# A hybrid GLA and convolution block on 8 cores: unequal halves of a sequence, with one plan of work for each half

## The reference

```python
p = h @ w_in[l]                                   # (B,S,IN_WIDTH)
q, k, v, g, lr, cb, cc, cx, ga, gb = jnp.split(p, SPLIT_IDX, axis=-1)
log_a = jax.nn.log_sigmoid((lr @ w_gate_up[l] + b_gate[l]).astype(jnp.float32)) / GATE_TAU
o = gla_chunked(qh, kh, vh, lah)                  # S_t = diag(a_t) S_{t-1} + k_t^T v_t ; o_t = q_t S_t
y_a = (rmsnorm(o, gla_norm_w[l]) * jax.nn.silu(g)) @ w_proj_a[l]
y_b = (cb * causal_depthwise_conv(cc * cx, conv_w[l])) @ w_proj_b[l]
z = jax.nn.sigmoid(ga) * y_a + jax.nn.sigmoid(gb) * y_b
x = x + gate1[:, None, :] * (z @ w_out[l])
m = jnp.square(jax.nn.relu(h2 @ w_mlp1[l])) @ w_mlp2[l]
x = x + gate2[:, None, :] * m
return rmsnorm(x, final_norm_w)
```

## Time and profile before

| | us |
|---|---|
| median of 3 runs | 1322.65 (1319.77 to 1343.83) |
| profiled execution | 1321.02 |
| its span, slowest core (5) | 1319.5 |
| spans of all cores | 1312.9 to 1319.5 |
| PE busy | 1250.9 (95%) |
| DVE, ACT, POOL busy | 751.3, 441.7, 89.4 |

### The profile page before, as it was taken

One profiled execution on the slowest core, in us unless ns is written; L12 is line 12 of the kernel. 1 busy time (PEld: TensorE's weight loads), 2 busy tenths in 40 slices (PEclk: granted clock), 3 DMA queues, 4 the chain that ended last, 5 costly groups with the idle time before them and its releaser, 6 DMA issues.

```text
span 1319.5 us, 19276 instructions; the slowest of 8 cores (1312.9 to 1319.5 us)
## 1 busy us (share of the span) xinstructions
PE 1250.9 (95%) x6772; PEld 611.2 (46%) x6772; DVE 751.3 (57%) x1203; ACT 441.7 (33%) x936; POOL 89.4 (7%) x133
## 2 busy tenths in 40 slices
PE   1588999999999999999999999999999999999996
PEld 1244565555554444444444444444444444444443
DVE  2468627767666565433232326676665556655786
ACT  2576526766431111331111113643111111112333
POOL 2000002244400000000000000000000000000000
PEclk9989999999999999999999999999999999999998
DMA  9568401001645353411113146004303023031122
GB/s 178 135 172 234 129 14 65 1 1 42 104 73 97 69 108 73 88 32 33 33 34 61 34 112 208 0 1 80 64 0 65 15 50 64 1 64 33 65 96 96
DMA packets 18173, 93.19 MB, mean 71 GB/s; under 512 B 2352, under 2 KB 2448, under 8 KB 12192
## 3 DMA queue, kind: packets, MB, share of 16 engines
q0 software_dynamic: 8208, 54.56, 22.8%
q1 hardware_dynamic: 9728, 37.14, 8.0%
q10 hardware_dynamic: 144, 0.26, 0.1%
HBM read 135.93 MB, written 8.39 MB: 109 GB/s over the span
## 4 chain that ended last, share of the span: by engine, by line
PE 91%; DMA 3%; DVE 2%; ACT 2%; issue 2%; POOL 0%; DVEq 0%; ACTq 0%; POOLq 0%
PE psf L429 88%; DMA wsl<-w_ada 3%; PE psf L439 2%; ACT Bt L374 1%; DVE Bx L422 1%; ACT hT L415 0%; DVE tmp L381 0%; ACT hT L374 0%; ACT tmp L374 0%; DVE S L396 0%; DVE x L381 0%; DVE h32T L384 0%; DVE x L396 0%; POOL xb L498 0%; DVE scb L381 0%
## 5 line engine op out<-in xcount | busy, mean ns | idle before, releaser
L429 PE MATMUL psf<-hT,wsl 128*128 128x512 bf16 x2944 | 661.0, 380 | 2.5 <-ACT hT L415 1.7
L429 PEld LDWEIGHTS psf<-hT,wsl 128*128 128x128 bf16 x2944 | 287.4, 98 | 344.2 <-issue 9.4
L374 ACT ACTIVATE tmp<-psf 128x512 f32<-128x512 f32 (+1 forms) x232 | 135.1, 582 | 532.1 <-PE psf L429 530.8
L429 PE MATMUL psf<-wsl,aT 128*128 128x512 bf16 (+1 forms) x1032 | 225.7, 379 | 2.0 <-DVE aT L381 2.0
L429 PEld LDWEIGHTS psf<-wsl,aT 128*128 128x128 bf16 x1032 | 101.2, 98 | 123.6 <-issue 4.8
L381 DVE TENSOR_TENSOR aT<-tmp 128x512 bf16<-128x512 f32 x128 | 88.6, 692 | 118.5 <-ACT tmp L374 113.3
L381 DVE TENSOR_TENSOR tmp<-tmp,psf 128x512 f32<-128x512 f32 (+1 forms) x72 | 45.2, 628 | 152.9 <-ACT tmp L374 152.9
L381 DVE TENSOR_TENSOR x<-x,tmp 128x512 f32<-128x512 f32 (+1 forms) x161 | 110.7, 688 | 16.8 <-DVE tmp L381 2.9
L381 DVE TENSOR_TENSOR tmp<-psf,g2b 128x512 f32<-128x512 f32 x129 | 88.6, 687 | 30.8 <-PE psf L429 30.8
L390 POOL TENSOR_SCALAR S_bf<-S,dec 128x256 bf16<-128x256 f32 x60 | 56.6, 960 | 184.9 <-DVE S L396 184.8
L429 PE MATMUL psf<-ogT,wsl 128*128 128x512 bf16 x256 | 60.5, 379 | 0.0
(11 more groups left out here) (170 smaller groups left out, 1045.3 us busy)
## 6 DMA issues: line engine op xcount, KB each, us to landing
wsl<-w POOLq DMA_DIRECT2D x16, 1024.0 KB, 9.0
wsl<-w_ada POOLq DMA_DIRECT2D x12, 1024.0 KB, 11.6
xb<-x_cur SPq DMA_DIRECT2D x16, 512.0 KB, 5.9
wsl<-w_merge POOLq DMA_DIRECT2D x8, 1024.0 KB, 8.4
x<-x_cur SPq DMA_DIRECT2D x16, 512.0 KB, 11.3
out<-x SPq DMA_DIRECT2D x15, 512.0 KB, 2.6
xb<-x_prev SPq DMA_DIRECT2D x12, 512.0 KB, 6.3
wsl<-w_conv POOLq DMA_DIRECT2D x8, 768.0 KB, 12.3
```

Source lines behind the costliest of these rows:

```text
L374: P.op("act", lambda e: e.activation(out=out, in_=in_, func=func, **kw), r, w, cost=0.19 + 0.00083 * size(in_) + (0.2 if "accum_out" in kw ...
L429: ins = e.matmul(out=o, lhsT=l, rhs=rh, start=st, stop=sp_)
```

## The change

- The halves are 17 and 15 subtiles (`SUBS`). `x_cur`, `x_prev` and `out` have 17.
- `record` gets `first` and is called twice; each result is planned by itself, and each engine's program holds both. An engine loads the word `half` from memory into a register and branches: half 0 (cores 0, 2, 4, 6) runs the first plan, half 1 the second.
- First plan: 17 subtiles in tiles of 4, 4, 3, 3, 3. No pass over x_prev, no `s0_pieces`: the state and the convolution's edge are set to 0 by POOL. x_cur tile 0 is loaded in the place of x_prev tile 0. Four weight buffers. k and q come once, in float32, on POOL's queue behind the four ada weights, and are cast on the chip by 8 pieces each on ACT or DVE (`cast`). Subtile 0 keeps its float32 q, k and scores, and its bf16 columns are no longer computed. In tile 0 all k products stand ahead of all q products, and v comes last. x tile 1 is loaded on POOL's queue.
- Second plan: 15 subtiles in tiles of 4, 4, 4, 3, and a pass over 17 subtiles in tiles of 4, 4, 3, 3, 3. Five weight buffers. No float32 q and k. No multiplication with the flag.
- Matmuls and vector work have the tile's own width (512 or 384). Buffers of the tiles are laid out anew; x1 is one buffer a subtile.
- The planner's assumed costs: x 1.9 (1.7), weights 6.1 a full one (6.5), the bus free from 6.0, small DMAs off it; and where no operation can go on, one whose engine could be chosen may go to the other.
- The chains gates, ln and scan of the first tile go head by head, not in pairs.

```diff
-TOK = 2048
-NW = 5
+SUBS = (17, 15)
@@
-        bus = 0.0
+        bus = 6.0
+        stuck = False
...
+                if cost < 1.0:
+                    end = st + 2.2
+                else:
+                    bus = max(bus, st + 1.0) + cost
+                    end = bus + 1.0
@@
+        def record(P, place, first):
+            main = tiles((4, 4, 3, 3, 3) if first else (4, 4, 4, 3), False)
+            past = [] if first else tiles((4, 4, 3, 3, 3), True)
+            seq = past + main
+            NW = 4 if first else 5
...
+                if first and name in ("k", "q"):
+                    return
...
+            def cast(name):
+                j, w32 = (4, w32k) if name == "k" else (5, w32q)
+                keys = [("w", j % NW)] + [("cast", name, kc) for kc in range(8)]
+                for kc in range(8):
+                    AV(wsl[j % NW].t[:, kc * 512:(kc + 1) * 512], w32.t[:, kc, :],
+                       w32.k((kc * 512, 512)) + [("free", j % NW)], [keys[1 + kc]])
+                return keys
...
             for j in range(4):
                 rec_load(j)
-            rec_load(4)
+            if first:
+                for dst, name, sem in ((w32k, "k", "c6"), (w32q, "q", "c5")):
+                    P.op("pool", lambda e, dst=dst, name=name: e.dma_start(
+                        out=dst.t[:, :, :].rearrange("p k c -> p (k c)"), in_=W[name][0]), [], dst.k(), dma=sem, cost=6.1)
+            else:
+                rec_load(4)
...
-            xload(1, after=[("w", 3)])
+            if first:
+                done_w(4)
+                xload(seq[1], eng="pool")
+            else:
+                xload(seq[1], after=[("w", 3)])
...
+            if first:
+                wkk = cast("k")
+                special_front()
...
+                    MM([(p_[:, w0:w], wk_[:, kc, hs], h_.t[:, kc, w0:w], kc == 0, kc == 7) for kc in range(8)], wkk + h_.k(), pk)
...
+            if first:
+                P.op("pool", lambda e: e.memset(S32.t[:, :, :], 0.0), [], S32.k())
+                P.op("pool", lambda e: e.memset(S_bf[0].t[:, :, :], 0.0), [], S_bf[0].k())
+                run(dense(main[0]))
...
             run(w1_stage(0, 0))
+            for t in range(1, NT):
+                tr2(main[t])
+                if t + 1 < NT:
+                    o_stage(main[t + 1])
+                if t + 2 == NT:
+                    done_w(2)
+                if t < 3:
+                    run(w1_stage(0, t))
             P.op("sp", lambda e: e.dma_start(out=fnw.t[:, :], in_=fnwb_d), [], fnw.k(), dma="c4")
+            todo1 = [(0, t) for t in range(3, NT)] + [(qd, t) for qd in range(1, 4) for t in range(NT)]
+            todo2 = [(qd, t) for qd in range(4) for t in range(NT)]
+            run(w2_stage(*todo2.pop(0)))
+            while len(todo1) > 1:
+                run(w1_stage(*todo1.pop(0)))
+                while len(todo2) > len(todo1) + 1:
+                    run(w2_stage(*todo2.pop(0)))
...
+                half = e.value_load(half_d[0:1, 0:1])
+                with e.If(half == 0):
+                    go(progs[0])
+                with e.Else():
+                    go(progs[1])
```

More of the change, by code:

```diff
@@ L125, in schedule @@
                         other = engs[1 - engs.index(e)]
-                        if max(free[other], ready[i]) < st + (MARGIN if e == engs[1] else 0.0):
+                        if max(free[other], ready[i]) < st + (MARGIN if e == engs[1] else 0.0) and not stuck:
                             continue
@@ L239, in k, with __init__, tiles @@
         return out
+class Tile:
+    def __init__(self, i, s0, n, prev):
+        self.i, self.s0, self.n, self.w, self.prev = i, s0, n, 128 * n, prev
+def tiles(widths, prev):
+    out, s0 = [], 0
+    for i, n in enumerate(widths):
+        out.append(Tile(i, s0, n, prev))
+        s0 += n
+    return out
 def plan():
@@ new lines, in dense @@
+                if nn:
+                    out.append((0.01, lambda: xload(nn)))
+                tr = [tr_piece(nx, kc) for kc in range(8)] if nx else []
+                if not (first and T.i == 0):
+                    for h in range(4):
+                        out += [q_piece(T, h), k_piece(T, h), vs.pop(0), ktr(T.i % 2, h, T)]
+                        out += tr[2 * h:2 * h + 2] if T.i else []
+                out.append((0.01, lambda: done_w(2 if nx is None else 0)))
+                if nx is None:
+                    return out + vs
@@ new lines, in dense @@
+                gs = gate_pieces(nx)
+                norm = sq_pieces(nn) if nn else []
+                rest = (tr if T.i == 0 else []) + [lr_piece(nx)] + gs[0:2] + norm[0:2] + gs[2:4] + norm[2:]
+                k_ = max(1, (len(rest) + len(vs) - 1) // len(vs))
+                while vs or rest:
+                    out += rest[0:k_] + vs[0:1]
+                    rest, vs = rest[k_:], vs[1:]
+                return out + (xs_pieces(nn) if nn else [])
+            if first:
+                P.op("pool", lambda e: e.memset(S32.t[:, :, :], 0.0), [], S32.k())
+                P.op("pool", lambda e: e.memset(S_bf[0].t[:, :, :], 0.0), [], S_bf[0].k())
+                run(dense(main[0]))
+            else:
+                for j in range(len(past) - 1):
+                    Vtt(ks[:, :], ksp[:, 0:4] if j == 0 else ks[:, :], ksp[:, j * 4 + 4:j * 4 + 8], ALU.add,
+                        [("ksp", 0), ("ksp", j + 1), "ks"], ["ks"])
+                d0 = dense(main[0])
+                run(d0[0:12])
+                weave(d0[12:], s0_pieces())
@@ L1347, in build_nc @@
+        progs = []
+        for first in (True, False):
+            planned = Prog()
+            record(planned, None, first)
+            order, place = planned.schedule({"ps": (8, 1), "tmp": (NTMP, 1)})
+            P = Prog()
+            record(P, place, first)
+            P.emit_all(order)
+            progs.append(P)
+        sem_names = sorted(set(progs[0].sems()) | set(progs[1].sems()))
         S = {n: es.enter_context(nc.semaphore(n)) for n in sem_names}
```

767 lines of the change are left out of this document (396 added, 371 removed).

## The result

The changed kernel takes 1279.66 us (median of 4 executions, 1279.23 to 1301.8) against 1321.77 of the kernel before in the same comparison: a ratio of 0.969, 95% interval 0.967 to 0.971. The profiled execution took 1279.36 us, with a span of 1277.7 on core 6. The forecast was 1285, range 1270 to 1302, and a span of 1283.

A forecast was written before the change was run, and what follows sets the result against it. TensorE was taken as the bound: a first-half main part of 1225.9 us beginning at 56 gives 1281.9, plus 1 for the jump, span 1283; with 1.5 outside the span 1284.5, called 1285, range 1270 to 1302.

The forecast's parts named there:

- the main part of 1163.1: Kernel before, from the first q product of the own tokens at 156.37 us to the span's end, nearly pure PE.
- Start: First-half opening: branch 2.5 us, hT ready at 46.8, first k product at 51, main part in effect from 56.
- the 5 us for half clock and first waits: First-half start: 5 us (0 to 12) added because the main part no longer begins with all weights there.
- Steps 1 to 5: First-half main part: 40.5 us stays, 16.6 goes, 1106.0 grows by 17/16 (+69.1), dropped columns -3.5, extra matmuls +1.3.
- Step 6: Tile boundaries in q, k, v and GLA: narrow tiles cover the vector chain less, +4 us (0 to 19).
- R1: Rival: vector chain bounds q, k, v and GLA with narrow tiles, 4.7 us a boundary, +15, 1300; chance 0.12.
- Step 7: MLP, first quarter: with four weight buffers one w2 load waiting for w_out's buffers is exposed, +8.5 us (0 to 14).
- R3: Rival: slower than before, four buffers uncover the MLP loads, six more exposures of 8.5 us, +51, 1336; chance 0.06.
- Jump at the end: End of the first-half program: 1 us for jumping over the other plan.
- The second half: Second-half cores: pass 117 us, main part from 169 lasting 1079, end at 1248, hidden behind the first half.
- the bound of 3.8: Start on every core: upper end for the register load and branch, two constants' landings, range 0 to 3.8 us.

The follow-up runs named there:

- the casts: Changed kernel with the pieces of the k and q casts alternating between ACT and DVE, q's after the first tile's scans: ratio 0.961, profiled first-half mean 1272.9 us.
- two gains: Changed kernel with both the alternating casts and the second half's start held by eight POOL fills: ratio 0.964, profiled first-half mean 1272.0 us.
- plans exchanged: Changed kernel with the two plans in swapped places in the program, each core doing the same work: ratio 0.972, profiled first-half mean 1287.3 us.
- held core 5: Second-half core of the changed kernel with the second half's first x request held by eight POOL fills: ratio 0.965, profiled first-half mean 1273.3 us.

## Why the prediction was right, and where it wasn't

The structure held: first-half cores set the end, the main part of 1163.1 grows by a sixteenth of what depends on tokens, and begins some 103 us earlier. The span of 1283 was 5.3 too long. By the steps:

- **Start.** Register and near branch cost 1.5 us (0 to 3.8, taken 2.5). hT was ready at 42.2, not 46.8: I kept the 37.9 us from the x request (1.57 to 39.48), and it became 34.2 because the neighbour core asks later. k landed 4.6 earlier for the same reason (6.4 us behind the fourth weight, where I took 6.5), but its cast took 7, not 2.5 (one engine instead of two), so the first k product came at 52.15 against 51. Two errors cancelled. Of the 5 us for half clock and first waits behind it, about 1.3 came (granted 0.97 over 45 us).
- **Steps 1 to 5** held. Two weight requests in the merge are now 29.41 us apart (491.47 and 520.88), and 27.62 x 17/16 is 29.35. 64 of 384 columns take 10.40 (807.24 to 817.64), 162.5 ns each, against my 163.
- **Step 6.** 6.2 us of waits in this stretch, against 5.2 (the 1.2 of before and 4 for the boundaries). It comes to 1.5 a boundary and not 4.7, so R1 didn't come. What I missed is which tiles make it: it is the run of 3-wide tiles, and 4,4,4,3,2 has 2.1. With the clock behind the waits and the tail, that run cost this change 8 us.
- **Step 7 is the step that fell.** 8.5 us for an exposed w2 load; measured 0. The release of an aT buffer gates only the vector product that writes it, so 40 matmuls of the next stage were free to move ahead, the end of my range that I gave to the planner. With them held back the kernel is 5 to 6 us longer, about what the step priced, but the wait was for the norm chain, which the step doesn't have. R3, which multiplied this step, had nothing under it: PE was busy 410.00 of 410.00 us in the MLP.
- **Jump at the end.** 1 us was allowed and 1.2 came, inside the span: 4.3 us from the last store request to its end, against 3.1 on far cores. The far branch itself, of which the prediction said that no run showed it, was left without a price at the second half's start.
- **The second half.** Main part from 169.59, predicted 169, end 1250.3, predicted 1248; but by two errors of the same size. Its start came 7.5 later (54.27 against 46.8), since the far branch is outside the bound of 3.8 that I set from the landing of the constants, and its pass took 115.3 us, not 122.2. Had the second half set the end, that bound would have been a costly one.

Working back from 1282.9: the start 2.5 less, step 7 8.5 less, step 6 1.0 more, the tail with the jump 0.2 more (10.5 against 9.3 + 1), makes 1273.1; the span is 1277.7. Of the 4.6 between them 1.7 is the granted clock of 0.83 from 210 to 220 us. The other 2.9 stay open. So the nearness of 1283 is in part luck: 11 us too much at the start and in step 7 stand against 4.6 that no step had.

## What to carry to other kernels

Give uneven work when one half of the cores has a prologue that the others don't need, and price the unit that moves (here some 70 us) before choosing the split: equal halves took 0.5% off the time, uneven ones 3.1%. When a buffer comes free late, look at which instruction of the consuming stage is gated; if it isn't the matmul, a planner that looks ahead can cover the load. Choose tile widths by the chains that run beside them: three tiles of 3 in a row cost 8 us more here than a 3 and a 2 at the end. And judge differences of 2 to 4 us by all executions: the profiled one alone put the casts 1 us too high, and hid that two gains nearly add.

## What the runs showed of the hardware

- **Far branch.** With both plans in one program, cores that take the first one ask for x at 3.0 to 3.3 us, the others at 9.7 to 11.8 (changed kernel and plans exchanged); the near ones take 1.2 us more from the last store request to the end. In sum the order is worth 10.5 us. The plan that sets the time belongs first.
- **Neighbours share what memory delivers.** The same loads take 36.3 to 37.9 us with both cores in step and 29.8 to 31.4 when one is 17 to 20 us ahead. The held core 5 asked 12.8 us later, ended its loads 8.7 later, and the second half ended 6 later, which costs nothing while it has 27 us of slack.
- **A short wait can cost more than its length.** Behind a wait of 4.50 us 24 transposes took 2.72 us instead of 1.50 (the window 830 to 835 was granted 0.69); behind one of 2.29 the last group took 1.7 us more in one profile of a kernel and not in another.
